# Attention inside a two-layer encoder trunk: the row maxima directly behind the scaling, the normalisation behind them and in two halves of four heads

## The reference, cut to what matters

```python
lc = jnp.einsum('bcqgrd,bckgd->bgrcqk', qc, kb).astype(f32) * scale + bias
lc = jnp.where(valid[:, None, :], lc, NEG_INF)
pc = softmax_with_sink(lc, sink[:, :, None, None, None])
oc = jnp.einsum('bgrcqk,bckgd->bcqgrd', pc.astype(v.dtype), vb).reshape(B, S, G, R, Dh)
```

## Time and profile before

| what | value |
|---|---|
| median of three executions | 2217.56 us |
| the profiled execution's own time | 2215.72 us |
| span of the profile | 2213.9 us |
| granted TensorE clock, mean over the span | 0.99 |
| share of the span: TensorE, VectorE, ScalarE, GpSimd | 96%, 49%, 37%, 21% |

### The profile page before, as it was taken

How to read it: one execution, slowest core, us unless ns; L and a number is a source line. 1 busy time by engine, 2 the same in 40 slices (tenths; PEclk the granted TensorE clock), 3 DMA queues, 4 the chain that set the end, 5 groups by cost and what they waited for, 6 DMA issues and landing times.

```text
span 2213.9 us, 50941 instructions
## 1 busy us (share of the span) xinstructions
PE 2128.2 (96%) x22780; PEld 1837.6 (83%) x22780; DVE 1082.0 (49%) x1532; ACT 810.4 (37%) x1389; POOL 475.1 (21%) x597
## 2 busy tenths in 40 slices
PE   7999999999899998999999999999999889999997
PEld 6888888777799976788888888888888677888886
DVE  5433324857766656843342373333255648433323
ACT  4333322566233352543332253333232545333310
POOL 2111111440142224511110131111033415111112
PEclk9999999999999999999999999999999999999999
DMA  4322321321000012232232123233213112322311
GB/s 165 132 98 103 132 84 46 109 77 39 13 4 4 4 62 94 82 115 96 96 132 98 39 94 118 96 110 120 78 56 97 48 39 77 134 96 103 131 53 39
DMA packets 29098, 183.43 MB, mean 83 GB/s; under 512 B 3232, under 2 KB 8160, under 8 KB 9936
## 3 DMA queue, kind: packets, MB, share of 16 engines
q1 hardware_dynamic: 28032, 178.79, 23.0%
q0 software_dynamic: 848, 1.37, 0.3%
HBM read 174.31 MB, written 4.30 MB: 81 GB/s over the span
## 4 chain that ended last, share of the span: by engine, by line
PE 82%; DVE 12%; ACT 4%; issue 1%; POOL 1%; DMA 0%; SPq 0%; POOLq 0%; ACTq 0%; DVEq 0%
PE psum L289 69%; PE psum L1660 6%; DVE arena L357 2%; PE psum L1651 1%; DVE arena L405 1%; PE psum L383 1%; ACT arena L2598 1%; PE psum L1684 1%; DVE arena L395 1%; POOL arena L480 1%; PE psum L2389 1%; DVE split L264 1%; DVE arena L2669 1%; DVE arena L331 0%; DVE h L362 0%
## 5 line engine op out<-in xcount | busy, mean ns | idle before, releaser
L289 PE MATMUL psum<-x,split 128*128 128x256 f16 (+1 forms) x5568 | 637.4, 276 | 8.6 <-POOL x L424 7.1
L289 PEld LDWEIGHTS psum<-x,split 128*128 128x128 f16 x5568 | 542.9, 98 | 99.0 <-issue 14.3
L289 PE MATMUL psum<-x,split_more 128*128 128x256 f16 (+1 forms) x2496 | 286.4, 276 | 3.7 <-POOL x L424 2.2
L739 POOL TENSOR_TENSOR arena<-arena 128x256 f16<-128x256 f32 (+1 forms) x176 | 120.5, 685 | 787.3 <-ACT arena L576 787.3
L289 PE MATMUL psum<-x,arena 128*128 128x256 f16 (+2 forms) x2448 | 281.9, 276 | 5.0 <-POOL x L991 3.5
L289 PEld LDWEIGHTS psum<-x,split_more 128*128 128x128 f16 x2496 | 244.0, 98 | 40.7 <-issue 3.6
L289 PEld LDWEIGHTS psum<-x,arena 128*128 128x128 f16 (+1 forms) x2448 | 240.0, 98 | 41.6 <-POOL x L991 5.6
L264 DVE SCALAR_TENSOR_TENSOR split<-stage,split 128x2048 f16<-128x2048 f32 (+1 forms) x77 | 189.9, 2466 | 157.5 <-ACT split L258 157.5
L289 PE MATMUL psum<-arena,split 128*128 128x256 f16 (+1 forms) x2304 | 260.9, 275 | 0.0
L289 PEld LDWEIGHTS psum<-arena,split 128*128 128x128 f16 x2304 | 225.1, 98 | 34.5 <-issue 2.2
L659 DVE SCALAR_TENSOR_TENSOR arena<-psum,arena 128x256 f32<-128x256 f32 (+1 forms) x176 | 75.5, 429 | 312.0 <-ACT arena L570 307.4
(11 more groups left out here) (221 smaller groups left out, 2506.8 us busy)
## 6 DMA issues: line engine op xcount, KB each, us to landing
stage<-in_w_gu SPq DMA_DIRECT2D x88, 1024.0 KB, 4.9
stage<-in_w_down SPq DMA_DIRECT2D x32, 1408.0 KB, 6.1
stage<-in_w_rkv SPq DMA_DIRECT2D x12, 1024.0 KB, 4.9
stage<-in_w_out SPq DMA_DIRECT2D x4, 1024.0 KB, 5.1
stage<-in_w_q SPq DMA_DIRECT2D x4, 1024.0 KB, 4.8
stage<-in_w_o SPq DMA_DIRECT2D x4, 1024.0 KB, 5.9
h_spill<-h SPq DMA_DIRECT2D x1, 2112.0 KB, 12.0
out<-h SPq DMA_DIRECT2D x8, 256.0 KB, 2.1
```

Source lines behind the costliest of these rows:

```text
L289: last = pe.matmul(o, wt(wp, k), xs(xp, k), start=(k == 0 and wp == 0 and xp == 0), stop=(k == tiles - 1 and wp == 1))
L739: e.tensor_tensor(hid[s][:, 1, m, 0:n], hid32[:, no % 2, 0:n], hid[s][:, 0, m, 0:n], ALU.subtract).then_inc(hid_lo, 1)
```

## The change

VectorE's loop becomes scored(i+1), maxima(i+1), normed(i), rest(i-2). `normed` works on units 0 to 3 and then on units 4 to 7, each half with its own sum, reciprocal and multiplication; its first half waits for the first four exponentials (step p0), its second for all (p1). TensorE's `turned` waits for the half that it reads before each of its four groups. Nothing is changed in `pool`, and no DMA is moved.

```diff
-            a_act = Steps(sem("softmax_act"), ["es", "p"])
-            n_dve = Steps(sem("softmax_dve"), ["den", "rd", "p"])
+            a_act = Steps(sem("softmax_act"), ["es", "p0", "p1"])
+            n_dve = Steps(sem("softmax_dve"), ["den0", "rd0", "p0", "den1", "rd1", "p1"])
...
                 def turned(i):
                     s, nb = i % 2, keys(i)
-                    e.wait_ge(n_dve.sem, n_dve.count("p", i))
                     for name, b0, rows, c0, n in (("tb", 3, nb, META, nb), ("tm", 5, META, 0, META)):
                         for h2 in range(2):
+                            e.wait_ge(n_dve.sem, n_dve.count(f"p{h2}", i))
                             after(e, t_act2, name, i - 1)
...
-                    ins.then_inc(a_act.sem, a_act.step("p"))
+                        if u % 4 == 3:
+                            ins.then_inc(a_act.sem, a_act.step(f"p{u // 4}"))
...
                 def normed(i):
                     s, nb = i % 2, keys(i)
                     es, rs, rd = stats(i, "es", "rs", "rd")
-                    e.wait_ge(a_act.sem, a_act.count("p", i))
-                    e.tensor_tensor(rd, rs, es, ALU.add).then_inc(n_dve.sem, n_dve.step("den"))
...
+                    for f in range(2):
+                        u = slice(4 * f, 4 * f + 4)
+                        e.wait_ge(a_act.sem, a_act.count(f"p{f}", i))
+                        e.tensor_tensor(rd[:, u], rs[:, u], es[:, u], ALU.add).then_inc(n_dve.sem, n_dve.step(f"den{f}"))
+                        e.wait_ge(n_dve.sem, n_dve.count(f"den{f}", i))
+                        e.reciprocal(rd[:, u], rd[:, u]).then_inc(n_dve.sem, n_dve.step(f"rd{f}"))
+                        e.wait_ge(n_dve.sem, n_dve.count(f"rd{f}", i))
+                        pr = prob[:, s, u, 0:META + nb]
+                        e.tensor_tensor(pr, pr, rd[:, u].unsqueeze(2).to_broadcast([P, 4, META + nb]), ALU.mult).then_inc(
+                            n_dve.sem, n_dve.step(f"p{f}"))
...
                     if i + 1 < NCH:
                         scored(i + 1)
-                    normed(i)
                     if i + 1 < NCH:
                         maxima(i + 1)
+                    normed(i)
                     if i >= 2:
                         rest(i - 2)
```

## The result

The changed kernel took 2222.43 us in the median of 20 executions (2216.39 to 2225.39), the kernel before 2216.26 (2212.42 to 2218.49, 20 executions): ratio 1.0028, 95% interval 1.0022 to 1.0034. That is +6.2 us, within the range given and just inside the 0.3% that counts as no change; the interval lies above 1, so it is a small loss. The forecast was +2.7. The profiled execution took 2224.16 us (span 2222.4).

The account below looks back on a forecast made before the run. The prediction took a VectorE-ScalarE loop of 7.13 us a chunk to bound the changed stage (TensorE the whole span). Opening +0.95, middle +1.73 and end 0 gave +2.7 on 2217.56: about 2220.3 us, range 2212.5 to 2226.5.

Parts of the forecast that it names:

- what is late next: With the exponentials freed, VectorE's scaling waits for TensorE's transposes: a loop of 7.32 us a chunk instead of 7.13.
- the tm1 wait: scored(i+2) overwrites the `prob` slot that chunk i's transposes read, so it waits for the last; about 1.1 us idle.
- Rival A: Transposes don't hold VectorE, whose own work bounds at 6.17 us a chunk: -4.0 us, 2213.6, at best 2210.5; chance 0.06.
- contention: GpSimd copies slow VectorE's maxima and normalisation beside them: about 1.05 us a burst, 3.15 for three in the middle.
- A burst: GpSimd copies of about 4 us after a values product, falling on VectorE's maxima and normalisation; three expected in the middle.
- the sum: Opening +0.95, middle +1.73 (5 x 7.32 + 3.15 against 38.02) and end 0: +2.7 us in all.
- Rival D: Every two-input VectorE operation of a burst waits for a copy, 3.7 us a burst: +10.6 us, 2228; chance 0.05.
- Rival B: GpSimd's slowing of VectorE stays as before, 2.37 us in the middle, none in the opening: +0.6 us, 2218.2; chance 0.22.
- the opening: Up to scored(2): 0.55 us late from the new order and halves plus 0.4 for one multiplication's loss, together 0.95.
- the clock in the middle: TensorE's granted clock from 1736 to 1776, 1.00 before, was taken to stay there and given no term.
- rival C: TensorE's clock falls in the middle chunks, each loop about 1.0 us longer, six times: +8.7 us, 2226.3; chance 0.09.
- The end: From scored(7) to values(6): 12.9 us instead of 13.82, the 0.9 gain set against about 1.0 of lower clock: zero.

Follow-up runs that it names:

- Order alone: Kernel before with only VectorE's order changed (maxima before normalisation), normalisation whole: 2220.26 us against 2216.28, ratio 1.0020.
- halves alone: Changed kernel with VectorE's old order (normalisation, then maxima), so only the split normalisation is taken over: 2213.03 us, ratio 0.9986 to the kernel before.
- three slots: `prob` given a third slot: in the changed kernel 2210.53 us (loop 6.33); with only the order changed, normalisation whole, 2205.44 us (loop 5.80).
- the profile with the multiplications: Changed kernel with 12 small, thrown-away TensorE multiplications ahead of each chunk's transposes: 2219.71 us, ratio 1.0016 to the kernel before.

## Why the prediction was right, and its size too small

**Right: what is late next.** The new loop through the tm1 wait was forecast at 7.32 us and measured at 7.31, the idle time ahead of the scaling at 1.1 and measured at 1.08, a half multiplication at 0.76 and measured at 0.76. Order alone, halves alone and three slots each gave their loop: 7.30 (7.27 expected), 6.50 (6.53), 6.33 (6.3) and 5.80 (5.8 to 5.9). The last transposes waited for ScalarE's copies, as forecast (1.7 us). Rival A, that the transposes don't hold VectorE, is what three slots make true.

**Nearly right: contention.** A burst was priced at 1.05. The loop with one at the full clock took 8.18, 0.87 more than 7.31, and leaving out three bursts with the clock held gave 2.9 us, 1.0 each. The parts were 0.37 of a half multiplication and 0.34 of a small step of the maxima, as priced (0.41 and 0.34), but 0.09 of a sum instead of 0.31. In the changed kernel's profile only two bursts cost anything, 1.74 us instead of the 3.15 of the sum: the third fell into the 4.30 us that VectorE waited for TensorE. Rival D falls: the term is not three times as large. Rival B was wrong in the opening; in the middle its 2.37 us and the 2.88 of three measured bursts lie too close to tell apart.

**Too small: the opening.** 0.95 was forecast. This execution reached the stage 2.03 us late, before any changed instruction (first scores at 1725.23 instead of 1723.20); less that, scored(2) came at 1736.50 against 1734.81, 1.69 late. I had allowed one loss by contention, 0.4. There were three: a small step of the maxima took 0.48 instead of 0.17, and in the second half of chunk 0 the sum took 0.56 instead of 0.15 and the multiplication 0.93 instead of 0.53.

**Wrong in size: the clock in the middle.** The step that failed is the one that took the middle at the full clock, put the clock at nothing in the sum and gave rival C 0.09, because the busy share of 31/40 would stay. It did stay, 32.26 of 40 us, some of it work at the lower level; but the granted clock of 1736 to 1776 was 0.83 in the profiled execution. By the prediction's own sign ("if the granted clock of the middle is below 1.00") it was wrong here. That the time lies in the range is owed to this rival too: the range was drawn to take in C, and by size the measured +6.2 lies nearer to C's +8.7 than to the +2.7 of the sum. The forecast time, 2220.3 us, looks nearer (2.1 us off) by luck: the median of three that it started from lay 1.3 us above that of twenty. The loops were 0.84, 3.26 and 1.28 us over 7.31 or 8.18, together 5.4. C was priced at 1.0 in each of six chunks; it came in three, and harder in one of them, since at the lower level values and scores also overran the gap.

**The end.** values(6) started 1794.89 - 1782.20 = 12.69 us after scored(7), forecast 12.9 at the full clock. The transposes of chunk 6 were not at the lower level this time, so the gain of 1.13 on 13.82 stayed; I had set it off against 1.0.

**The sum.** To the first multiplication of the projection (1804.48 instead of 1796.10, +8.38): 2.03 late start, 1.69 opening, 43.67 - 38.02 = 5.65 in the middle, -1.13 and +0.14 at the end. The execution was 2224.16 - 2215.72 = 8.44 longer. Over the medians it is +6.2. Executions at the same mean clock help to tell the parts apart (means in us, in brackets the number of executions; the last column is the difference):

| granted clock of the execution | before (of 69) | after (of 20) | difference |
|---|---|---|---|
| 0.992 | 2214.7 (11) | 2216.6 (3) | +1.9 |
| 0.991 | 2216.2 (15) | 2217.9 (1) | +1.7 |
| 0.989 | 2217.6 (12) | 2220.7 (2) | +3.1 |

So what the forecast priced, 2.7, is 2 to 3 us. The table rests on few executions, and its clock is that of the whole span and not of the stage; but the profile with the multiplications, whose middle was at 1.00, gives the same, 75.13 - 72.90 = 2.2 us for the stage. The rest, some 3.5 us, goes with a clock of 0.9877 instead of 0.9907. That the gaps of TensorE in the changed kernel have to do with the lower level is shown by the multiplications that filled them: with them the middle was at 1.00 and the time 2.7 us lower. Why the clock fell in these chunks and not in others of the same shape stays open: in the changed kernel it fell behind gaps of 1.66 and 0.42 us (1741.48 to 1743.14 and 1743.80 to 1744.22), and in the kernel before it stayed at 1.00 behind one of 2.45.

## What to carry to other kernels

Before an instruction is moved ahead of another, ask which wait the moved one had been covering: here the maxima hid the transposes that hold a two-slot buffer, and moving them exchanged a loop of 7.13 us for one of 7.30. Where two loops have nearly the same length, breaking one of them gives nothing: order alone cost 4.0 us, and with the third slot, which breaks the other, it gave 10.8. Halving a step paid only while it lay in the loop (-3.3 us by itself, +5.1 once it didn't, part of that perhaps by the clock). And a TensorE product that comes onto another engine's path brings its clock with it, so the clock needs a term in the sum.

## What the runs showed of the hardware that was not expected

What the lower clock costs depends on what waits for TensorE. In the kernel before, the 16 transposes of chunk 6 took 3.38 us instead of 1.97 and the exponentials hid it. In the changed kernel twelve transposes took 1.53, 2.38 or 2.81 us, and two loops grew by just that much (0.84 and 1.28 us). It can also cost behind the stage that was changed: 1.96 us in the projection of order alone.

Also, the reduction of the maxima was not delayed by GpSimd's copies in the changed kernel (1.35 us in all seven chunks, with and without them), while sums and multiplications with two inputs were, from 0.15 to 0.56 and from 0.76 to 1.13 us.
